# A hybrid decoder layer: the operands of the next pair of heads are made between the solve steps of this pair

## The reference

```python
w = -softplus(-(w0 + tanh(w_lo) @ w2)) - 0.5;  decay = exp(-exp(w))
a = sigmoid(a0 + a_lo @ a2);  g = sigmoid(g_lo) @ g2
kk = k * k_k;  k = k * (1 + (a - 1) * k_a)
kk = kk / max(sqrt(sum(kk * kk, per head)), 1e-12)
def step(S, ...):                      # S is 64 x 64 per head
    sa = S @ -kk_t
    S = S * w_t + outer(sa, kk_t * a_t) + outer(v_t, k_t)
    return S, S @ r_t
out = (group_norm(o) + sum(r * k * r_k) * v) * g
```

## Time and profile before

| | us |
|---|---|
| median of 3 runs | 3486.49 |
| lowest and highest | 3480.80, 3487.53 |
| the profiled execution, its own time | 3483.44 |
| its span, from the first instruction to the last | 3481.8 |
| TensorE busy | 3249.2 |
| VectorE busy | 1490.5 |
| ScalarE busy | 536.9 |
| GpSimd busy | 251.9 |

### The profile page before, as it was taken

One profiled execution on the slowest core, in us unless ns is written; L12 is line 12 of the kernel. 1 busy time (PEld: TensorE's weight loads), 2 busy tenths in 40 slices (PEclk: granted clock), 3 DMA queues, 4 the chain that ended last, 5 costly groups with the idle time before them and its releaser, 6 DMA issues.

```text
span 3481.8 us, 52140 instructions
## 1 busy us (share of the span) xinstructions
PE 3249.2 (93%) x21602; PEld 2619.5 (75%) x21602; DVE 1490.5 (43%) x2473; ACT 536.9 (15%) x1086; POOL 251.9 (7%) x489
## 2 busy tenths in 40 slices
PE   8999988889988877789799999999999999999997
PEld 6888777777764455557588888888888877888886
DVE  1111255554996523333634343343343443444457
ACT  1000133331313322220200000000000001000012
POOL 0000011110000233430000000000000000000000
PEclk9999988989998988899899999999999999999998
DMA  5222100003210266772123322333233323222232
GB/s 154 73 73 73 37 10 9 9 7 84 61 44 6 89 183 201 234 217 63 54 80 85 85 77 82 84 85 85 73 85 85 85 64 91 82 83 82 79 96 74
DMA packets 446357, 289.26 MB, mean 83 GB/s; under 512 B 22937, under 2 KB 434054, under 8 KB 444728
## 3 DMA queue, kind: packets, MB, share of 16 engines
q1 hardware_dynamic: 431940, 246.80, 25.1%
q0 software_dynamic: 14192, 39.21, 3.6%
HBM read 275.46 MB, written 10.49 MB: 82 GB/s over the span
## 4 chain that ended last, share of the span: by engine, by line
PE 82%; DVE 7%; issue 3%; ACT 3%; SPq 2%; DMA 1%; POOL 1%; POOLq 0%; DVEq 0%; ACTq 0%
PE ps L999 47%; PE ps L565 16%; PE ps L620 7%; PE ps L844 4%; PE ps L980 3%; PE ps L832 1%; PE ps L807 1%; POOL W L374 1%; SPq L437 1%; PE ps L810 1%; SPq L374 1%; DMA W<-in_cache_k_dram 1%; DMA W<-in_w_in_dram 0%; ACT BIG L1195 0%; PE ps L901 0%
## 5 line engine op out<-in xcount | busy, mean ns | idle before, releaser
L565 PE MATMUL ps<-XT,W 128*128 128x272 f32 (+1 forms) x2496 | 578.4, 394 | 1.8 <-DMA W<-in_w_in_dram 1.2
L565 PEld LDWEIGHTS ps<-XT,W 128*128 128x128 f32 (+1 forms) x2496 | 471.2, 189 | 110.4 <-issue 5.7
L999 PE MATMUL ps<-XT,W 128*128 128x272 f32 x1408 | 339.1, 394 | 18.4 <-ACT XT L1272 17.8
L999 PE MATMUL ps<-XT,SUMS 128*128 128x272 f32 x1408 | 337.0, 392 | 0.0
L999 PEld LDWEIGHTS ps<-XT,W 128*128 128x128 f32 x1408 | 268.7, 191 | 74.8 <-issue 18.2
L999 PEld LDWEIGHTS ps<-XT,SUMS 128*128 128x128 f32 x1408 | 267.5, 190 | 55.1
L1786 DVE TENSOR_TENSOR U2B<-ps,S1B 128x272 f32<-128x272 f32 x76 | 33.5, 440 | 616.4 <-PE ps L999 616.4
L999 PE MATMUL ps<-TD,W 128*128 128x272 f32 x704 | 173.5, 395 | 5.4 <-DVE TD L1700 4.3
L999 PE MATMUL ps<-BIG,SUMD 128*128 128x272 f32 x704 | 172.0, 393 | 4.2 <-ACT S5B L1300 4.2
L999 PE MATMUL ps<-BIG,W 128*128 128x272 f32 x704 | 172.2, 393 | 2.4 <-ACT CNB L1278 2.4
L999 PE MATMUL ps<-T4U,W 128*128 128x272 f32 x704 | 170.3, 395 | 2.9 <-DVE T4U L1700 2.9
(11 more groups left out here) (356 smaller groups left out, 4323.7 us busy)
## 6 DMA issues: line engine op xcount, KB each, us to landing
W<-in_w_up_dram SPq DMA_DIRECT2D x176, 512.0 KB, 5.1
W<-in_w_in_dram SPq DMA_DIRECT2D x38, 1024.0 KB, 5.7
W<-in_w_down_dram SPq DMA_DIRECT2D x64, 384.0 KB, 4.2
W<-in_w_down_dram SPq DMA_DIRECT2D x64, 320.0 KB, 3.6
W<-in_cache_k_dram POOLq DMA_DIRECT2D x128, 128.0 KB, 3.5
W<-in_cache_k_dram SPq DMA_DIRECT2D x128, 128.0 KB, 3.3
W<-in_cache_v_dram POOLq DMA_DIRECT2D x128, 128.0 KB, 3.0
W<-in_cache_v_dram SPq DMA_DIRECT2D x128, 128.0 KB, 2.5
```

The source lines that it names most:

```text
L565: last = nc.tensor.matmul(ps[0:width, 2 * acc + h, 0:HALF], wt[u][:, k, 0:width], XT[:, k, h * HALF:(h + 1) * HALF], start=k == 0, stop=k ...
L999: last = nc.tensor.matmul(ps[:, bank, 0:HALF], weights[:, k * P:(k + 1) * P], x[:, k], start=start and k == 0, stop=k == kc - 1, skip_grou ...
```

## The change

Pair 0's setup is done ahead of the loop. In the loop, while pair p is solved, the setup of pair p + 1 is issued in pieces between the steps. On TensorE the generator `ahead` gives six pieces, one behind each of the first six steps: decay, rate, norm sums, gate, bonus sums, sample transposes. All of them write banks 6 and 7, so each waits until the one before has been evacuated. ScalarE and VectorE have their parts as functions which are called between the solve's evacuations, and VectorE's operands are made in four halves, one behind each of the first four state scalings. GpSimd makes its operands behind the copies of the pair ahead, and fetches the low-rank weights two pairs ahead. The decays at the chunks' ends go to a small tile of their own (`PXE`, two buffers). The second half's transition products are interleaved with the first state and output terms. The state's final transpose goes to bank 5 instead of 6, and the wait for the last output copy moves into the next pair.

```diff
         WKV = carve(CHUNK)
...
             BOTH = range(2)
 
-            for p in range(PAIRS):
-                pe.wait_ge(S["lw_landed"], 64 * p + 64)
-                if p == 1:
-                    pe.wait_ge(last_ev, 3)
-                halves = [slice(h * HALF, (h + 1) * HALF) for h in BOTH]
+            halves = [slice(h * HALF, (h + 1) * HALF) for h in BOTH]
+
+            def ahead(q):
+
+                pe.wait_ge(S["lw_landed"], 64 * q + 64)
                 for h in BOTH:
...
+                yield
+                pe.wait_ge(S["lora_ev"], 3 * q + 1)
                 for h in BOTH:
-                    last = nc.tensor.matmul(ps[:, 2 + h, 0:HALF], LW[64:128, 0], ZT[64:128, 36, halves[h]], start=True, stop=True)
+                    last = nc.tensor.matmul(ps[:, 6 + h, 0:HALF], LW[64:128, 0], ZT[64:128, 36, halves[h]], start=True, stop=True)
                 last.then_inc(S["lora_mm"], 1)
-                pe.wait_ge(S["sq_ready"], p + 1)
+                yield
+                pe.wait_ge(S["lora_ev"], 3 * q + 2)
+                pe.wait_ge(S["sq_ready"], q + 1)
                 for h in BOTH:
                     last = nc.tensor.matmul(ps[:, 6 + h, 0:HALF], headsum, SQ[:, halves[h]], start=True, stop=True)
                 last.then_inc(S["ss_mm"], 1)
...
                 for h in BOTH:
-                    nc.tensor.matmul(ps[:, 4 + h, 0:HALF], LW[:, 1], ZT[:, 37, halves[h]], start=True, stop=False)
-                    last = nc.tensor.matmul(ps[:, 4 + h, 0:HALF], LW[0:32, 2], ZT[0:32, 38, halves[h]], start=False, stop=True)
+                    nc.tensor.matmul(ps[:, 6 + h, 0:HALF], LW[:, 1], ZT[:, 37, halves[h]], start=True, stop=False)
+                    last = nc.tensor.matmul(ps[:, 6 + h, 0:HALF], LW[0:32, 2], ZT[0:32, 38, halves[h]], start=False, stop=True)
                 last.then_inc(S["lora_mm"], 1)
-                pe.wait_ge(S["bonus_in"], p + 1)
+                yield
+                pe.wait_ge(S["lora_ev"], 3 * q + 3)
+                pe.wait_ge(S["bonus_in"], q + 1)
                 for h in BOTH:
-                    last = nc.tensor.matmul(ps[:, 6 + h, 0:HALF], headsum, BON[:, h * HALF:(h + 1) * HALF], start=True, stop=True)
+                    last = nc.tensor.matmul(ps[:, 6 + h, 0:HALF], headsum, BON[:, halves[h]], start=True, stop=True)
                 last.then_inc(S["bonus_mm"], 1)
...
+                yield
+                pe.wait_ge(S["bonus_ev"], q + 1)
+                pe.wait_ge(S["ab_ready"], q + 1)
+                pe.wait_ge(S["exp_ev"], 4 * q + 4)
                 for j in range(6):
                     src = SVT6[:, j * N_DEC:(j + 1) * N_DEC]
-                    last = nc.tensor.transpose(ps[0:N_DEC, j // 4, (j % 4) * P:(j % 4) * P + P], src, ident)
+                    last = nc.tensor.transpose(ps[0:N_DEC, 6 + j // 4, (j % 4) * P:(j % 4) * P + P], src, ident)
                 last.then_inc(S["sv_mm"], 1)
+                yield
+            for _ in ahead(0):
+                pass
+            for p in range(PAIRS):
+                pieces = ahead(p + 1) if p + 1 < PAIRS else iter(())
...
                 def each_head(bank, at, width, lhsT, rhs, start=True, stop=True, cross=False):
@@ -639,6 +652,11 @@
                     for half, bank in enumerate((6, 7)):
                         if s:
                             pe.wait_ge(S["tok_ev"], 4 * p + 1 + half)
+                            if p and half == 0:
+                                pe.wait_ge(S["o_ev"], 2 * p)
+                                pe.wait_ge(S["wkv_ev"], p)
+                            if p == 1 and half == 0:
+                                pe.wait_ge(last_ev, 3)
                         tokens = by_token(1 - s, bank)
                         for g_last in gram(s, (2 * half, 2 * half + 1)):
                             t_last = next(tokens)
...
+                next(pieces, None)
...
                     pe.wait_ge(S["s3_ev"], 2 * n)
...
+                next(pieces, None)
...
                     products(s, [(3 * s, 0, 64, lambda c: N4[s][:, c], lambda c: P2T[s][:, c])])
+                next(pieces, None)
...
+                next(pieces, None)
...
+                next(pieces, None)
...
+                next(pieces, None)
...
-                for s in BOTH:
-                    n = 2 * p + s + 1
-                    pe.wait_ge(S["solve_dve"], after("solve_dve", "b3", n, s))
-                    products(s, [(3 * s + 2, 0, 128, lambda c: TB[s][:, 0, c], lambda c: TB[s][:, 2:4, c])], cross=s == 1)
...
+                def transition(s):
+                    for c in range(SC):
+                        yield each_head(3 * s + 2, c * 128, 128, TB[s][:, 0, c], TB[s][:, 2:4, c], cross=s == 1)
+                pe.wait_ge(S["solve_dve"], after("solve_dve", "b3", 2 * p + 1, 0))
+                for last in transition(0):
+                    pass
+                last.then_inc(S["solve_pe"], 1)
+                pe.wait_ge(S["solve_dve"], after("solve_dve", "b3", 2 * p + 2, 1))
+                crossed = transition(1)
+                if p + 1 < PAIRS:
+                    pe.wait_ge(S["sv_ev"], p + 2)
+                for g in range(2):
+                    next(crossed)
+                    state_alone(g)
+                    last = next(crossed)
+                    if g:
+                        last.then_inc(S["solve_pe"], 1)
+                    out_alone(g)
                 pe.wait_ge(S["solve_dve"], after("solve_dve", "g", 2 * p + 1, 0))
-                for g in range(2):
-                    state_alone(g)
-                    out_alone(g)
...
                 pe.wait_ge(S["chain_ev"], 8 * p + 9)
-                each_head(6, 0, CHUNK, ST[0], id64).then_inc(S["wkv_mm"], 1)
+                each_head(5, 0, CHUNK, ST[0], id64).then_inc(S["wkv_mm"], 1)
                 if p == 0:
                     pe.wait_ge(S["o_ev"], 2)
+                    pe.wait_ge(S["wkv_ev"], 1)
                     for r in range(9):
                         last = nc.tensor.transpose(ps[0:RW_TILES, 3 + r // 4, r % 4 * P:(r % 4 + 1) * P], LAST_IN[:, :, r], ident)
                     last.then_inc(last_mm, 1)
-                pe.wait_ge(S["o_ev"], 2 * p + 2)
+                pe.wait_ge(S["o_ev"], 2 * p + 1)
+            pe.wait_ge(S["o_ev"], 2 * PAIRS)
...
+            def decay_raw(q):
+                act.wait_ge(S["lora_mm"], 3 * q + 2)
+                nc.scalar.activation(two(LD), ps[:, 6:8, 0:HALF], ACT.Tanh, bias=HB[:, q:q + 1], scale=0.5).then_inc(S["lora_ev"], 1)
...
+            def rate_raw(q):
+                act.wait_ge(S["lora_mm"], 3 * q + 3)
+                act.wait_ge(S["bd_dve"], q)
+                nc.scalar.activation(two(AA), ps[:, 6:8, 0:HALF], ACT.Tanh, bias=HB[:, 8 + q:9 + q], scale=0.5).then_inc(S["lora_ev"], 1)
+
+            def root(q):
+                act.wait_ge(S["ss_max"], q + 1)
...
+            def decays(q):
+                act.wait_ge(S["lprev_ready"], q + 1)
+                act.wait_ge(S["bd_pool"], q)
+                nc.scalar.activation(PXE[q % 2], LC[:, CHUNK - 1:SEQ:CHUNK], ACT.Exp)
                 nc.scalar.activation(PY[:, 0:SEQ], PY[:, 0:SEQ], ACT.Exp).then_inc(S["exp_ev"], 1)
                 nc.scalar.activation(PN[:, 0:SEQ], LC[:, 0:SEQ], ACT.Exp, scale=-1.0).then_inc(S["exp_ev"], 1)
                 nc.scalar.activation(PX[:, 0:SEQ], LC[:, 0:SEQ], ACT.Exp).then_inc(S["exp_ev"], 1)
...
+            def gate(q):
+                act.wait_ge(S["lora_mm"], 3 * q + 4)
+                act.wait_ge(S["pair_pool"], q + 1)
+                nc.scalar.activation(two(G), ps[:, 6:8, 0:HALF], ACT.Copy).then_inc(S["lora_ev"], 1)
+
+            def sample_vectors(q):
+                act.wait_ge(S["sv_mm"], q + 1)
+                act.wait_ge(S["sv_out"], 16 * q + 16)
                 sv = SVT[0:N_DEC].rearrange("p a n -> p (a n)")
-                nc.scalar.activation(sv[:, 0:512], ps[0:N_DEC, 0, :], ACT.Copy)
-                nc.scalar.activation(sv[:, 512:768], ps[0:N_DEC, 1, 0:256], ACT.Copy).then_inc(S["sv_ev"], 1)
+                nc.scalar.activation(sv[:, 0:512], ps[0:N_DEC, 6, :], ACT.Copy)
+                nc.scalar.activation(sv[:, 512:768], ps[0:N_DEC, 7, 0:256], ACT.Copy).then_inc(S["sv_ev"], 1)
...
+                if more:
+                    square_kk(p + 1)
...
                     nc.scalar.activation(NN[s], bank(3 * s), ACT.Copy).then_inc(S["s3_ev"], 1)
                     nc.scalar.activation(TB[s][:, 1], bank(3 * s + 1)[:, 0], ACT.Copy).then_inc(S["s3_ev"], 1)
+                if more:
+                    decay_raw(p + 1)
+                    rate_raw(p + 1)
+                    root(p + 1)
                 for s in BOTH:
                     act.wait_ge(S["solve_pe"], after("solve_pe", "m", 2 * p + s + 1, s))
...
                     nc.scalar.activation(MM[s], bank(3 * s + 1), ACT.Copy).then_inc(S["solve_act"], 1)
+                if more:
+                    decays(p + 1)
+                    gate(p + 1)
...
```

(68 more changed lines are left out.)

73 lines of the change are left out of this document (33 added, 40 removed).

## The result

| | before | after |
|---|---|---|
| median of 4 runs (one more before than above), us | 3486.69 | 3439.70 |
| lowest and highest | 3480.80, 3487.53 | 3433.04, 3440.21 |
| ratio of times, 95% interval | | 0.9863, 0.9851 to 0.9876 |
| profiled execution, its own time | 3483.44 | 3439.39 |
| its span | 3481.8 | 3437.7 |

The kernel is 47.0 us faster (3486.69 - 3439.70). I had forecast 67.4 us, that is 3419, with a range of 3400 to 3448. The direction and the mechanism hold, the range holds the time, and the forecast is 20.7 us too low.

What follows compares the result with a forecast made beforehand. Bound: the recurrent stage, 393.3 us, with a 13.3 us setup gap per pair. Forecast stage 19.3 + 40.2 + 40.3 + 193.5 + 32.6 = 325.9, a gain of 67.4 us: 3419 us, range 3400 to 3448.

Steps and rivals of the forecast that it cites:

- gap of 13.3 us: Setup ahead of each pair's first gram product, with TensorE mostly waiting on VectorE and ScalarE; claimed removed, 13.3 us.
- 9.7 x 0.85: Gram products and first squaring: 9.7 us at clock 0.85, claimed to take 8.2 at full clock.
- Together 6.3 us per pair: Six pieces added to TensorE's queue: 24 records at 0.23 us (5.6) plus sample transposes (0.7), all on the path.
- bound from above, 12.6: Upper bound on the six pieces' cost per pair, were all at the low clock: 12.6 us.
- I take 0.4 gained: Second transition product interleaved with first state and output terms in other quadrants: 0.4 us gained per pair, bounds 0 to 0.9.
- charged 0.5: VectorE's half-width operands in the chain, two of them colliding with GpSimd's product: 0.5 us per pair, bounds 0 and 1.2.
- my 18.9: Length of the solve in pair 3 before the change, 18.9 us, with TensorE busy 18.26; base of the 24.1.
- The timetable of the other engines: VectorE and ScalarE work between solve steps claimed ready before TensorE needs it: no charge, 0.2 us to spare before b3.
- Two other signs: Signs of the profile after: VectorE's idle before By and B sums gone; wrong if chain steps beyond the second exceed 0.8 us.
- The rival of stalls: Pieces stall the solve because VectorE or ScalarE is late: 4.1 us per pair, 29 in all, 3448; chance 0.14.
- 19.3 + 40.2: Pair 0: serial setup on two shared banks 19.3 us (15.7 plus 3.6), then 40.2 with gram products at low clock.
- granted clock of 1.00 in every pair but the first: Sign of the profile after: gram products start within 1 us of the last state scaling, at full clock except in pair 0.

Runs made afterwards that it cites:

- kernel in order: Kernel after the change, with the second half's transition products in one row and the first state and output terms behind them: 3438.6 us, ratio 0.9879.
- kernel with banks of its own: Kernel after the change, with pair 0's setup on the banks it had before and without its waits on evacuations: 3431.6 us, ratio 0.9857.
- second profile: Kernel after the change, run and profiled once more with no edit: median 3435.8 us, ratio 0.9862, stage 346.7 us.
- two kernels with spares together and apart: Kernel after the change plus four unread products per pair, in a row behind the bonus piece (3444.3 us) or singly between solve products (3454.7 us).
- 9 and 8: Kernel before the change, with 9 spare products ahead of the bonus sums and 8 behind the sample transposes: 3478.1 us, ratio 0.9982.
- 19 and 16: Kernel before the change, with 19 spare products ahead of the bonus sums and 16 behind the sample transposes: 3481.3 us, ratio 0.9991.

## Why the prediction was right, and where its size was off

The stage came out at 350.4 us where I had summed 325.9: 24.5 us more. Pair 3, with no low clock and one idle time of 0.3 us in its gram products, from its first gram product (580.86) to the next pair's (621.78):

| term | forecast | measured |
|---|---|---|
| gram products and first squaring | 8.2 | 8.25 |
| decay piece to first scaling | 24.1 | 25.8 |
| chain | 5.4 + 0.5 | 6.3 |
| last scaling to next gram product | 0.5 | 0.56 |
| period | 38.7 | 40.9 |

- **The gap of 13.3 us is gone**, as forecast, and the gram stretch at full clock is 8.25 us, to 0.05 what 9.7 x 0.85 gave.
- **The step that failed: "Together 6.3 us per pair".** I priced the six pieces by their records alone. From the start of each to the next solve product the rows give 1.11, 1.12, 1.12, 2.6, 1.11 and 0.76, together 7.8; with 0.10 ahead of each and 0.05 behind the first product after it that is 8.7. The missing 2.4 us are the passages between the 64 x 64 form of the solve and the full width of the pieces (up to 0.34 each, six times) and the gate's three changes between 128-row and 32-row weights (0.19 each). My bound from above, 12.6, held it for another reason (the clock). The sum lacked a term for "small product, large product, small product"; the trace of before had only one such passage in each direction per pair, with waits beside it. The gate's part, however, stood in the trace of before, in pair 3's setup at full clock:

```profile
576.68 0.72 PE L597 MATMUL ps<-BIG 32*128 32x272 f32 x2
577.33 0.72 PE L596 MATMUL ps<-BIG 128*128 128x272 f32 x2
577.99 0.72 PE L597 MATMUL ps<-BIG 32*128 32x272 f32 x2
```

Two records every 0.65 us, where 2 x 0.23 is 0.46. I had priced them by the mean of another group.

- **"I take 0.4 gained" for the interleaving:** 0.0 through the quadrants, shown by the kernel in order. The gain was in the other half of that edit, which the prediction doesn't name: the terms no longer wait for VectorE's copy.
- **The chain: charged 0.5, measured 0.9**, within my bounds of 0 and 1.2. I had spread the contention over two halves at 0.66; it fell on one half, at 1.52.
- **Against these stands 1.1 us the other way** between the decay piece and the first scaling: 24.1 + 2.4 + 0.4 would be 26.9, and 25.8 was measured. It lies behind the first B3 sum, where the first scaling comes after 3.37 us and came after 4.45 in pair 3 before. 0.7 of it goes with the moved wait; the other 0.4 is a stretch that pair 3 alone had before, and on pair 3 my 18.9 rested. That the solve's sum is 1.7 us short and not 2.8 is luck: two terms that I didn't have went against the two that I had wrong.
- **The timetable of the other engines held.** I had warned of 0.2 us to spare for VectorE at the b2 place. The sums there start at 608.98, straight behind the bonus product (608.34, 0.72), so they do wait in VectorE's queue, which I had named as a sign of being wrong; but TensorE is busy 12.00 of 12.00 us around them, so it costs nothing. Two other signs were badly chosen. VectorE's idle time before the B sums isn't gone (1.41 and 1.12 us before the first two), and one step of the chain takes 1.1 us, from the third scaling to the fourth, but it did so before the change as well. The rival of stalls (3448) has nothing for it.
- **Pair 0: forecast 19.3 + 40.2, measured 64.7.** The setup grew by 5.6 us rather than 3.6, of which the serial banks are 4.6 by the kernel with banks of its own, and the low clock lasted until 456.5.

Summed over the stage: 2.2 us in each of seven pairs make 15.4, pair 0's setup 2.0, and 7.1 us are left (3.4 by the second profile's stage of 346.7). They are short stretches, most of them in the gram products of some pairs. The windows of the kernel after show one of two kinds, shortly after a pair has begun:

```profile
538.40:541.80 3.40, 3.40 (x93) 3.40 (x93) 0.46 (x2) 0.82 (x2) 0.00 (x0) 0.50 0.19 43
663.60:667.00 3.40, 3.40 (x176) 3.40 (x172) 1.60 (x4) 1.34 (x3) 0.00 (x0) 1.00 0.19 43
```

At 538.4 the clock is 0.50 with TensorE busy throughout, and 93 records pass where at 663.6, in the same place of another pair, 176 do: 1.6 us lost. In front of both lies the chain, in which TensorE is busy 4.07 of 6.00 us. So "a granted clock of 1.00 in every pair but the first" was wrong for two pairs of seven here; the other is the last one, with 0.54 from 746.9 to 750.3. In the second profile only the last pair has it (0.59 from 737.3 to 740.7). Which pairs are hit changes from run to run, and what decides it stays open.

The other kind is idle time inside the gram products. The chain of waits of the kernel after, at the pair that begins at 663.6:

```profile
663.47 4.61 PE ps L633 x152
668.09 0.57 issue
668.65 3.30 PE ps L633 x105
```

No semaphore and no engine releases this. In the second profile the same pair has it at the same place, 4.5 us behind its clearing, for 0.54 us; the next pair has 0.79 and 0.35 us at 3.1 behind its clearing in both. So it belongs to a place in the program, not to chance. The waits of the stage, from 440 to 820 us, have six times of this kind:

```profile
PE ps L633 <- issue: 3.5, 6, 1.0
```

That is 3.5 us in all, 2.5 in the second profile and 0.2, one time, in the kernel before. The DMA queues show what comes ahead of each. The view of 666.3 to 667.3 us holds one packet:

```profile
q8 instruction: 1, 0.02, 6.0%
```

It is 16 KB of a queue named instruction; it starts at 666.32, lands at 667.28, and TensorE goes on at 668.65, 1.37 us later. In the gram products such packets come every 3.5 to 5 us. Over the stage in all twelve profiles, each of TensorE's 59 idle times over 0.12 us without a releaser ends 1.2 to 1.6 us after such a packet has landed. So TensorE very likely waits there for its own instructions, of which it uses most in the gram products (228 records in the 4.6 us from 581.0, against 207 in the 12.0 from 600.0). No run tried this. With the 3 us or so that the two low stretches cost, it accounts for most of the 7.1, though some of these times only take the place of a wait for VectorE's masks.

## What to carry to other kernels

Work moved into another stage's in-order queue costs more than its records: if it has another tile form than its neighbours, add one passage (here 0.34 us) for each place where it is spliced in, and splice in few large pieces rather than many small, as the two kernels with spares together and apart show. A moved wait can be worth more than the overlap for which the code was moved: look at what stands ahead of each wait, before and after. Place two-input SBUF work of VectorE by what GpSimd is doing at that moment, not by the mean free time. And when a shared resource is made serial for the steady state, look at the first iteration, which has nothing to hide behind and may have banks to spare.

## What the runs showed that I had not expected

- A passage from 64 x 64 products to a full-width one and back costs 0.34 us at full clock, 0.10 ahead and 0.20 to 0.24 behind, with no wait in the trace; changing between 128-row and 32-row weights costs 0.2 us per change, and did so in the kernel before.
- VectorE's product of two SBUF operands took 1.52 us instead of 0.41 beside a GpSimd product of 1.27: it was held for 1.11 of the 1.24 us in which they met.
- Spare products in the idle time of the kernel before raised the clock in the stretch behind (0.50 to 1.00). With 9 and 8 it was low instead for 3.4 us at the start of the next setup, though TensorE does more in all; with 19 and 16 it was not, but they took as long themselves.
- TensorE's idle times without a releaser end 1.2 to 1.6 us after a 16 KB packet of its instruction queue has landed, every one of them.
